# A hybrid convolution and attention block on one core: the latent input is loaded and normed later, and the modulation rows are copied at once

## The reference

```python
def ada_mod(cond, w, b):
    m = jax.nn.silu(cond) @ w + b
    return jnp.split(m[..., None, :], N_MOD, axis=-1)

def conformer_conv(h, w_pw1, b_pw1, w_dw, b_dw, ln_g, ln_b, w_pw2, b_pw2):
    u = h @ w_pw1 + b_pw1
    a, g = jnp.split(u, 2, axis=-1)
    u = a * jax.nn.sigmoid(g)
    u = depthwise_conv(u, w_dw) + b_dw          # 31 taps
    u = jax.nn.silu(layer_norm(u, ln_g, ln_b))
    return u @ w_pw2 + b_pw2

# layer 0, start:
a_lat = modulate(rms_norm(x, mix_pre_g[i]), sh1, sc1)
a_ctx = modulate(rms_norm(h_ctx, mix_pre_g[i]), csh1, csc1)
y_lat, y_ctx = conformer_conv(a_lat, *cv), conformer_conv(a_ctx, *cv)
```

## Time and profile before

| what | us |
|---|---|
| median of 3 runs | 1771.61 (1770.87 to 1772.88) |
| the profiled execution | 1773.7 |
| its span in the trace | 1771.9 |
| TensorE matmul busy | 1641.7 (93%) |
| GpSimd, ScalarE, VectorE busy | 788.1, 754.0, 708.9 |

### The profile page before, as it was taken

How to read it: one execution, slowest core, us unless ns; L and a number is a source line. 1 busy time by engine, 2 the same in 40 slices (tenths; PEclk the granted TensorE clock), 3 DMA queues, 4 the chain that set the end, 5 groups by cost and what they waited for, 6 DMA issues and landing times.

```text
span 1771.9 us, 26331 instructions
## 1 busy us (share of the span) xinstructions
PE 1641.7 (93%) x9469; PEld 1302.6 (74%) x9469; DVE 708.9 (40%) x1396; ACT 754.0 (43%) x1136; POOL 788.1 (44%) x436
## 2 busy tenths in 40 slices
PE   5588998899899999999999799999987999999996
PEld 1466565678799988888888677787865788888884
DVE  2454677546663034433443524433342433332002
ACT  2422243546676444444422344444444444443220
POOL 0443333555678944434455324323326244444551
PEclk9789999999899999999999799999998899999998
DMA  8576768443456633322585111211203133233321
GB/s 307 189 209 180 233 202 240 167 142 119 142 157 188 191 94 95 95 87 91 190 291 184 50 37 42 69 57 42 66 25 107 48 95 95 95 95 88 97 77 48
DMA packets 70942, 222.63 MB, mean 126 GB/s; under 512 B 7888, under 2 KB 15568, under 8 KB 70608
## 3 DMA queue, kind: packets, MB, share of 16 engines
q1 hardware_dynamic: 69712, 217.81, 39.4%
q10 hardware_dynamic: 1152, 3.75, 0.5%
HBM read 216.03 MB, written 5.51 MB: 125 GB/s over the span
## 4 chain that ended last, share of the span: by engine, by line
PE 80%; issue 7%; DVE 6%; ACT 3%; DMA 2%; POOL 1%; DVEq 1%; ACTq 0%; SPq 0%; POOLq 0%
PE bank L1513 20%; PE bank L1514 19%; PE bank L1515 19%; PE bank L1723 3%; PE bank L1483 3%; PE bank L1724 3%; PE bank L1725 3%; PE bank L1801 2%; PE bank L1823 1%; PE bank L1457 1%; PE bank L1811 1%; DVE bank L1216 1%; PE bank L1653 1%; PE bank L1528 1%; ACT w_hi L756 1%
## 5 line engine op out<-in xcount | busy, mean ns | idle before, releaser
L609 POOL TENSOR_TENSOR w_lo<-w_raw,w_hi 128x1024 fp32r<-128x1024 f32 (+1 forms) x284 | 666.5, 2353 | 840.0 <-ACT w_hi L756 839.9
L756 ACT ACTIVATE w_hi<-w_raw 128x1024 fp32r<-128x1024 f32 (+1 forms) x284 | 294.7, 1038 | 229.3 <-PE bank L1515 200.2
L1513 PE MATMUL bank<-h_hi_lat,w_hi 128*128 128x512 f32 x888 | 354.7, 399 | 5.1 <-DVE h_lo_lat L1175 4.6
L1515 PE MATMUL bank<-h_hi_lat,w_lo 128*128 128x512 f32 x888 | 351.9, 396 | 0.0
L1514 PE MATMUL bank<-h_lo_lat,w_hi 128*128 128x512 f32 x888 | 351.9, 396 | 0.0
L1513 PEld LDWEIGHTS bank<-h_hi_lat,w_hi 128*128 128x128 f32 x888 | 167.4, 189 | 58.5 <-issue 10.7
L1515 PEld LDWEIGHTS bank<-h_hi_lat,w_lo 128*128 128x128 f32 x888 | 167.3, 188 | 41.0
L1514 PEld LDWEIGHTS bank<-h_lo_lat,w_hi 128*128 128x128 f32 x888 | 167.3, 188 | 39.8
L1513 PE MATMUL bank<-h_hi_ctx,w_hi 128*128 128x256 f32 x560 | 164.7, 294 | 20.4 <-DVE g_lo_ctx L1355 11.1
L1514 PE MATMUL bank<-h_lo_ctx,w_hi 128*128 128x256 f32 x560 | 160.6, 287 | 0.0
L1515 PE MATMUL bank<-h_hi_ctx,w_lo 128*128 128x256 f32 x560 | 160.6, 287 | 0.0
(11 more groups left out here) (192 smaller groups left out, 2693.9 us busy)
## 6 DMA issues: line engine op xcount, KB each, us to landing
w_raw<-in_ffn_w_up SPq DMA_DIRECT2D x132, 512.0 KB, 3.6
ada_raw<-in_mod_w SPq DMA_DIRECT2D x64, 512.0 KB, 5.6
w_raw<-in_cv_w_pw SPq DMA_DIRECT2D x48, 512.0 KB, 5.2
w_raw<-in_ffn_w_down SPq DMA_DIRECT2D x48, 448.0 KB, 3.4
mod_rows<-in_mod_rows SPq DMA_DIRECT2D x32, 512.0 KB, 5.4
w_raw<-in_ffn_w_down SPq DMA_DIRECT2D x24, 512.0 KB, 3.6
w_raw<-in_na_w_qkv SPq DMA_DIRECT2D x24, 512.0 KB, 5.7
shifted_lat<-u_lat SPq DMA_DIRECT2D x32, 270.0 KB, 6.5
```

The source lines that it names most:

```text
L609: pool.tensor_tensor(wlo[s][:, 0:kt * P], raw[s][:, 0:kt * P], whi[s][:, 0:kt * P].bitcast(F32), ALU.subtract).then_inc(w_lo, 1)
L756: act.activation(whi[s][:, 0:kt * P], raw[s][:, 0:kt * P], ACT.Copy).then_inc(w_hi, 1)
L1513: pe.matmul(b, whi[s][:, w], hi[:, a], start=(first and k == 0), stop=False)
L1515: ins = pe.matmul(b, wlo[s][:, w], hi[:, a], start=False, stop=(last and k == kts - 1))
```

## The change

Six edits, all in or before the 16 steps; the fourth holds for every chunk:

- `x` is no longer on ScalarE's queue behind `ctx`, but on SyncE's, behind chunk 0 and the weights of step 0, and ahead of the weights of step 1.
- `x`'s squares, which ScalarE computed right after `ctx`'s, come after the context's high parts and the weights of step 1. VectorE adds them pairwise in step 0, TensorE sums them in step 1 between the two halves, ScalarE takes the root and VectorE the reciprocal in step 1, and TensorE waits for that root before step 2 (`rms` 2).
- `x`'s tiles are now made in steps 1 to 6 by the table `in_l_at`: two in steps 3 and 6, one in the others. Low parts follow a step later.
- The rows of a chunk are copied in one activation of 128x512. For that the matmuls write 32 rows at each place instead of 2 (`cond` has the two conditions interleaved, with zeros behind them), and the clearing of `ada_row` goes.
- For chunk 0 this copy stands ahead of the first high parts; of these, two come before the context's high parts (`hi_h`) and two after.
- VectorE forms the context's low parts between its scalings instead of after all of them.

```diff
-            act.dma_start(X[LAT][:, :], x_t).then_inc(x_in, 16)
...
             step_loads(0)
+            sp.dma_start(X[LAT][:, :], x_t).then_inc(x_in, 16)
             step_loads(1)
...
+        in_l_at = {1: [0], 2: [1], 3: [2, 3], 4: [4], 5: [5], 6: [6, 7]}
...
             def ada_rows(c):
...
-                for g in range(4):
-                    r = slice(BLK32 * g, BLK32 * g + 2)
-                    ins = act.activation(ada_row[r, :], ADA_ACC[c][r, :], ACT.Copy)
-                ins.then_inc(row_out, 1)
+                act.activation(ada_row[:, :], ADA_ACC[c][:, :], ACT.Copy).then_inc(row_out, 1)
...
             in_fori(square_of, chains["in_c"])
-            act.wait_ge(x_in, 16)
-            in_fori(square_of, chains["in_l"])
-            lc = chains["ln_c"]
-            root(chains["in_c"], 1, RMS_EPS)
-            act.wait_ge(rms, 1)
-            root(chains["in_l"], 1, RMS_EPS)
-            act.wait_ge(row_z, 1)
-            hi_first(phases["pw1c"], None)
-            ada_rows(0)
-            in_fori(hi_h, chains["in_c"])
-            hi_h(chains["in_l"], 0, 0)
+            lc, in_l = chains["ln_c"], chains["in_l"]
+            root(chains["in_c"], 1, RMS_EPS)
+            ada_rows(0)
+            for j in range(2):
+                hi_of(phases["pw1c"], 0, j, True)
+            in_fori(hi_h, chains["in_c"])
+            for j in range(2, RING):
+                hi_of(phases["pw1c"], 0, j, True)
             act.wait_ge(x_in, 16)
+            in_fori(square_of, in_l)
+
+            def hi_in_l(n):
+
+                if n == 1:
+                    act.wait_ge(rms, 1)
+                    root(in_l, 1, RMS_EPS)
+                for t in in_l_at.get(n, ()):
+                    hi_h(in_l, t // 2, t % 2)
...
-            in_fori((scale_pair, chains["in_c"]), (lo_pair, chains["in_c"]))
-            in_l = chains["in_l"]
-            scale_pair(in_l, 0, (0,))
+            in_c, in_l = chains["in_c"], chains["in_l"]
+            scale_pair(in_c, 0)
+            for t in range(1, KD // 2):
+                scale_pair(in_c, t)
+                lo_pair(in_c, t - 1)
+            lo_pair(in_c, KD // 2 - 1)
             dve.wait_ge(u_pads, 4)
             for n in range(STEPS):
                 gated(n)
-                if n < KD:
-                    lo_pair(in_l, n // 2, (n % 2,))
-                if n < KD - 1:
-                    scale_pair(in_l, (n + 1) // 2, ((n + 1) % 2,))
+                if n == 0:
+                    in_fori((add_squares_pair, in_l))
+                elif n == 1:
+                    recip(in_l, 1)
+                for t in in_l_at.get(n - 1, ()):
+                    lo_pair(in_l, t // 2, (t % 2,))
+                for t in in_l_at.get(n, ()):
+                    scale_pair(in_l, t // 2, (t % 2,))
...
-                        ins = pe.matmul(ADA_ACC[c][BLK32 * g:BLK32 * g + 2, :], cond[:, k:2 * KD:KD],
+                        ins = pe.matmul(ADA_ACC[c][BLK32 * g:BLK32 * (g + 1), :], cond[:, 2 * k:2 * k + BLK32],
...
             stat_squares(chains["in_c"])
-            ada_products((0, CHUNK_BLOCKS // 2))
-            stat_squares(chains["in_l"])
-            ada_products((CHUNK_BLOCKS // 2, CHUNK_BLOCKS))
+            ada_products((0, CHUNK_BLOCKS))
...
-            extras = {KD + 2: lambda: stat_sum(lc, "conv_c"), KD + 3: ln_c_squares}
+            extras = {1: lambda: stat_squares(chains["in_l"]), KD + 2: lambda: stat_sum(lc, "conv_c"), KD + 3: ln_c_squares}
             for n in range(STEPS):
+                if n == 2:
+                    pe.wait_ge(rms, 2)
                 pw1_step(n, extras.get(n))
```

More of the change, by code:

```diff
@@ L177, in build @@
         ones = sb("ones", P)
-        cond = sb("cond", 2 * KD)
+        cond = sb("cond", 2 * KD - 2 + BLK32)
         acc = {LAT: sb("feature_sum_lat", L), CTX: sb("feature_sum_ctx", C)}
@@ L296, in build @@
         row_out = sem("row_out")
-        row_z = sem("row_z")
         ada_tr = sem("ada_tr")
@@ L598, in _ @@
             pool.memset(ones[:, :], 1.0).then_inc(ones_s, 1)
-            pool.memset(ada_row[:, :], 0.0).then_inc(row_z, 1)
+            pool.memset(cond[:, 2 * KD:], 0.0).then_inc(cond_s, 1)
             for side in (CTX, LAT):
@@ L799, in _ @@
             act.wait_ge(v_in, 16)
-            act.activation(cond[:, :], vec[:, at["c"]:at["c"] + 2 * KD], ACT.Silu).then_inc(cond_s, 1)
+            act.activation(cond[:, 0:2 * KD].rearrange("p (k i) -> p i k", i=2),
+                           vec[:, at["c"]:at["c"] + 2 * KD].rearrange("p (i k) -> p i k", i=2),
+                           ACT.Silu).then_inc(cond_s, 1)
             def ada_rows(c):
@@ L956, in _ @@
                     ada_rows(1)
-                glu_step(n, (lambda k=n + 1: hi_h(chains["in_l"], k // 2, k % 2)) if n < KD - 1 else None)
+                glu_step(n, lambda k=n: hi_in_l(k))
                 if n == KD + 2:
@@ L1250, in _ @@
             diag_weights(1)
-            in_fori((add_squares_pair, chains["in_l"]))
             recip(chains["in_c"], 1)
-            recip(chains["in_l"], 1)
             mod_add(0)
@@ L1663, in _ @@
             pe.wait_ge(ones_s, 1)
-            pe.wait_ge(cond_s, 1)
+            pe.wait_ge(cond_s, 2)
             lc = chains["ln_c"]
             stat_squares(chains["in_c"])
-            ada_products((0, CHUNK_BLOCKS // 2))
-            stat_squares(chains["in_l"])
-            ada_products((CHUNK_BLOCKS // 2, CHUNK_BLOCKS))
+            ada_products((0, CHUNK_BLOCKS))
             pe.wait_ge(cst_in, 64)
             ada_turn(0)
-            pe.wait_ge(rms, 2)
+            pe.wait_ge(rms, 1)
             def ln_c_squares():
```

## The result

The changed kernel takes 1748.78 us in the median of four runs (1744.28 to 1757.53), beside it the kernel before 1771.72. The ratio is 0.9876 with a 95% interval from 0.9853 to 0.9899. The forecast was 1762.3 with a range from 1758.5 to 1768.5: the sign was right, and the gain was more than twice the size forecast. The profiled execution took 1744.28 us, its span is 1742.5. It is the fastest of the four, so the two profiles lie 29.4 us apart where the medians lie 22.9 apart.

What follows compares the result with a forecast made beforehand. TensorE, busy 93% of the span, was taken as the bound, with savings only where it stands in the first 88 us. Steps 7.5 plus copies 1.8 gave 9.3: 1764.4, or 1762.3 against the median; range 1758.5 to 1768.5.

Steps and rivals of the forecast that it cites:

- 32 rows instead of 2. Columns and passes stay.: Matmuls on `mod_w`: weight loads of 32 columns cost 0 to 9.8 us more in all; 0 was taken.
- Chunk 0: Start, TensorE on `mod_w`: without `x`'s squares the last block is used by 40.4 instead of 42.74 us, bounds 39.0 to 42.74.
- chunk 0 ends no earlier: Rival: loads, not squares, set the pace at the start; all 2.3 us later, 7.0 gained, 1764.6 us; chance 0.10.
- Rows and modulation: Start: one copy of 0.59 us ends at 41.1, then 3.76 us unchanged to the first scaling, put at 44.6.
- Context tiles: VectorE's scalings and low parts at the start: 6.9 us plus 1.0 for meeting GpSimd, last ending at 52.5.
- The first sigmoid: ScalarE, step 0: sigmoid done at 60.6, `u` written at 61.3 instead of 66.86, winning 5.6 us.
- The first rival: The steps give half back: weights of step 2 late, sigmoid 3.6 us later, gain 4.2, 1767.4 us; chance 0.22.
- Step 1: TensorE starts at 61.2; `x`'s squares fill its 5.44 us gap; convolution takes 2.59, not 4.87, ending at 74.5.
- The second root: Steps 1 to 2: two extra table loads; `u` of step 2 written at 83.9, costing 2.5 us, winning 6.0.
- The round trip of step 2: Write of `u` to its reads, 5.58 us before: earlier-issued `mod_w` blocks are mostly drained, winning 0 to 2.9; 1.5 taken.
- `ada_rows(1)`: Copies of the next chunk's rows, TensorE's wait in step 10: three copies fewer win 1.8 us.
- the rival "slower": The two-step period breaks: each pair of steps gets a second wait, 8.5 us slower, 1780.1 us; chance 0.05.

Runs made afterwards that it cites:

- e2: The changed kernel with the wider `cond` moved to the end of memory, so all other tiles lie as in the kernel before: 1762.80 us, ratio 0.9950.
- e1: The kernel before with 128 unused bytes per partition behind `cond`, no instruction changed: 1759.83 us, ratio 0.9938.
- e4: The kernel before with 64 unused bytes behind `cond`, making the weights-to-activations distance 0 within 256 bytes: 1748.92 us, ratio 0.9872.
- e3: The changed kernel run again with no edit: 1748.31 us, ratio 0.9875 against the kernel before.
- e10: The kernel before with weights 192 and activations 256 bytes higher, so their distance is 0 within 256 bytes: 1748.83 us, ratio 0.9870.
- e9: A separate kernel where only TensorE works, 168 matmuls of 128x512 in each of twelve placements of weights and activations: 226.7 to 234.3 ns from start to start.
- e11: The kernel before, in its layout, with the single copy of 32 rows put ahead of the high parts and `x` loaded and normed as before: 1765.69 us, ratio 0.9962.

## Why the prediction was wrong, and where it was right

**The step that failed: "32 rows instead of 2. Columns and passes stay."** I costed the wider `cond` by its weight loads alone, between 0 and 9.8 us, and took 0. That part was fair: the matmuls of `mod_w` took hardly longer, 1.05 us for four (1.03 in the earlier trace rows), and e2, which has them, met the forecast. What I didn't cost is that the line which makes `cond` wider moves every tile behind it by 128 bytes. e1 measures that by itself: 10.5 us by the medians, 6.7 to 15.0 by the interval. My bounds for the edit had no value below nothing, so a gain had no place in the range. In the list of what would prove me wrong I named slower matmuls on `mod_w`, and never the pace of the matmuls in the phases that the change doesn't touch. With the term, 1762.3 - 10.5 is 1751.8, 3.0 above the result.

The three products before hold 3 x (888 + 352 + 168 + 40 + 32 + 24) = 4512 matmuls of 128x512. At 4.4 ns less each (e1) the most that could come is 20 us, and at 6.6 less (e4) 30. Measured are 10.5 and 21.4. The traces show where it came and where not. In the two latent feed-forward parts (614.43 to 985.94 and 1380.88 to 1752.43 before) TensorE hardly ever stands: there e4 wins 10.5 and 11.1 us, together all of its 21.4, and e1 7.0 and 6.5. The 1344 matmuls outside them brought nothing in sum, within an interval of some 4 us. One loss against them is in the same traces: the matmuls of 128x256 come slower in the new layouts. One context step's 48 go from first to last start in 5.45 us before (91.42 to 96.87), in 5.64 after (76.46 to 82.10) and in 5.74 in e4 (93.18 to 98.92). How the rest divides between this and waits for other engines was not measured.

**The moved work: right in sum.** 9.3 us forecast, 7.6 by the medians and 8.9 [5.8, 11.9] by the ratio in e2. That the sum came so close is in part luck, since its terms were off in both directions:

- *Chunk 0.* Forecast 40.4, measured 43.32. Here the rival "chunk 0 ends no earlier" was right, and I had given it one chance in ten. I took 1.27 us a block from a window in which 412 GB/s were drawn. In 22 to 42 us the kernel after draws less, and from 14 to 22 next to nothing:

```profile
14.00:22.00 8.00, 7.72 (x32) 4.76 (x31) 1.69 (x1) 3.21 (x8) 0.00 (x0) 1.00 0.06 4
22.00:42.00 20.00, 12.26 (x44) 1.72 (x44) 0.07 (x1) 0.00 (x0) 0.00 (x0) 0.91 0.94 326
```

  The ring's four blocks are full and TensorE is at the context's squares until 19.80, so no buffer comes free. Then twelve blocks of 0.52 MB, at 326 GB/s, need 19.3 us from about 22 on. Before, the load of `x` filled that hole:

```profile
14.00:22.00 8.00, 6.77 (x32) 4.06 (x31) 1.95 (x3) 5.70 (x14) 0.00 (x0) 1.00 0.43 157
22.00:42.00 20.00, 14.85 (x54) 2.50 (x56) 5.95 (x4) 2.53 (x4) 0.00 (x0) 0.91 0.90 332
```

  So `x` had ridden in time in which the queues stood, and its squares on TensorE had cost the loads next to nothing: 332 GB/s with them, 326 without. The other profiles scatter more than that (311 to 351 with, 336 to 356 without), but none has chunk 0 done by 40.4: in the five with the moved `x` it ends at 42.2 to 44.9. Why 326 and not 412 was not tried.

- *Rows and modulation.* One copy takes 0.60 (0.59 forecast) and stands ahead of the high parts. From its end, 43.97, to the first scaling at 47.47 are 3.5 (3.76). The forecast's 44.6 for that scaling is 0.2 to 0.3 short of its own terms.
- *Context tiles.* The low parts met GpSimd as forecast: the two from 49.04 took 1.29 us and ended at 50.3, 0.7 behind `w_lo`, which ran from 44.99 to 49.65. That cost 0.4 us (the next two took 0.87), not the 1.0 of the sum. The first product came at 50.08 (47.7). A second meeting I hadn't counted: the four additions of `x`'s squares took 4.67 us beside the `w_lo` of 60.50 and 63.24, one of them 2.86 and the others 0.68. By "Who interferes with whom" on the page "SBUF — State Buffer" of the Trainium skill the two exclude one another, and these rows agree. It cost nothing, as `rms` is needed much later.
- *The first sigmoid.* 61.74 against 60.1. The 2.9 us that chunk 0 came late shrank to 1.6 here; ScalarE was busy in front of it, and no wait for weights stands there. The first rival (half given back) therefore falls: its 3.6 us of late weights did not come.
- *Table loads.* The load of 60.45 ends at 61.73 and the sigmoid starts at 61.74; that of 74.33 ends at 75.61, the root starts at 75.62. By the drain that the Trainium skill gives on "ScalarE: Activation LUTs", "What ACT_TABLE_LOAD costs", each would have come 1.38 us later. These rows leave no room for it.
- *Step 1.* As forecast in kind: the squares fill the gap, and the convolution starts without a wait, at 73.73. It takes 2.80, as at the full clock, not 4.87; all five profiles with the moved `x` have this. It ends at 76.5 (74.5), as TensorE began the step at 62.95 (61.2), held by GpSimd's `w_lo`.
- *The second root.* Reciprocal at 76.24 (74.3), `u` of step 2 written at 85.45 (83.9). 4.4 us are won of 6.0.
- *The round trip of step 2.* Write to reads 4.72 us, 0.86 less than before; I took 1.5. The convolution starts at 95.30 (93.7), so 5.9 earlier instead of 7.5.
- *What made it up.* That convolution took 2.80 us where it took 4.48 before, 1.7 more that the sum didn't have. TensorE stood 3.03 us in front of it instead of 4.05. This isn't sure in every execution: in e3, the same kernel, it took 4.19 us behind a wait of 2.45, and in e10, with the order of before, 2.80 behind 3.33. A clock of 0.77 is granted in 100 to 104 us before, and 1.00 in 96 to 100 after:

```profile
100.00:104.00 4.00, 2.81 (x36) 1.91 (x40) 1.39 (x2) 2.03 (x3) 1.02 (x2) 0.77 0.97 321
```

```profile
96.00:100.00 4.00, 4.00 (x56) 3.18 (x49) 1.85 (x1) 1.40 (x3) 3.14 (x3) 1.00 1.02 293
```

- *`ada_rows(1)`.* 3.63 became 1.83 us: the 1.8 of the forecast to the hundredth. But the term was undersized: with the clock that no longer falls behind the wait, 3.3 us were won there.
- *The period.* It held. No step got a second wait, and the rival "slower" falls with it.

## What to carry to other kernels

When an edit changes the size of a tile, list which tiles move, and count a change of pace for every matmul that reads them, of either sign, before looking at the instructions that the edit names. A gain that keeps growing through phases that the change doesn't touch is a matter of layout until shown otherwise; count the matmuls in a stretch where TensorE never stands, in both kernels, and put the tiles back to tell it apart from the work. Price a wait of TensorE with the matmuls behind it: the 1.8 us of step 10 brought 1.5 more by the clock. And read the pace of a load from the stretch in which it will run, not from the best window of the trace: here 326 GB/s, not 412, and a transfer that seems to be in the way may be riding in time that nobody uses.

## What the runs showed of the hardware

- The pace of chained 128x512 matmuls at the full clock depends on the distance between the weights and the moving operand in the memory, within 256 bytes: 226.7 to 226.9 ns at distance 0, 228.9 at 64, 233.3 to 234.3 at 32, 96, 128, 160, 192 and 224. It is the same with every other engine and queue standing (e9). Only these distances were run.
- Matmuls of 128x256 gain nothing by it and lose a little: 48 of a context step take 5.45 us at distance 192, 5.64 at 64 and 5.74 at 0. The 528 on `g_hi_ctx` take 62.1 us at 192 and at 64 and 63.2 at 0, but 59.7 in e11, at 192 again, so something else counts for them as well.
- A wait of 3.63 us in step 10 was followed by a granted clock of 0.74 (206 to 210 us), one of 1.83 by 1.00 (194 to 198 us, after).
- 64 unused bytes were worth 21.4 us of 1770, as much as the whole change; both together 32.9.
